# Sums of squares for the norms: from GpSimd to ScalarE and VectorE in a two-part transformer block

## The chip, the cores and the metric

The program runs on one NeuronCore of a Trainium2 chip. The metric is the device time of one execution in microseconds, the median of several. Times below are microseconds (us) unless marked ns. PE is TensorE's matmul, PEld its weight load, DVE is VectorE, ACT is ScalarE, POOL is GpSimd, SP is SyncE, which only issues DMAs here.

## The reference

One sequence of 512 tokens with 1024 channels, in float32, goes through two blocks of two layers each. What matters here is the residual stream and the norm that follows every addition to it:

```python
def rms_norm(x, g):
    xf = x.astype(jnp.float32)
    y = xf * lax.rsqrt(jnp.mean(xf * xf, axis=-1, keepdims=True) + EPS)
    return (y * g.astype(jnp.float32)).astype(x.dtype)

# first block: convolution, feed-forward, attention, feed-forward
h = h + conformer_conv(h, ...)            # pw2 is its last product
h = h + swiglu_ffn(h, ...)                # ffn_out
h = h + nsa_attention(h, ...)             # w_o
h = h + swiglu_ffn(h, ...)
return rmsnorm(h, final_norm)
# second block, for each of two layers
h = rms_norm(x, g_mix[layer])
x = x + mixer(h, ...)                     # e_w_out in layer 0, o_w_out in layer 1
m = rms_norm(mem, g_mem[layer])
x = x + memory_cross_attention(rms_norm(x, g_xa[layer]), m, ...)   # xa_wo
x = x + swiglu(rms_norm(x, g_ffn[layer]), ...)                     # ffn2_out
```

## The kernel before, in words

The stream lies transposed in SBUF as `x`, eight tiles of 128 channels by 512 tokens. Float32 products are made of three float32r products (`three`): each operand is split into a high and a low part. A weight panel (128x1024) is loaded by SP into `raw`, ScalarE copies it into `wh` (L185), VectorE takes the rest into `wl` (L191). There are four panel slots, and the loads and splits run four panels ahead. Products go round a ring of four PSUM banks.

A `Residual` stage (L517) adds a product to the stream. TensorE makes eight products, one for each tile m. For tile m VectorE adds the PSUM bank to `x` (L644, with a bias L641), which frees the bank. ScalarE then writes `xh`, the high part of x times the next norm's gain (L620), and the high part of the panels that lie four ahead (L185). VectorE makes these panels' low part (L191) and last `xl`, the low part of x (L649). `xh` and `xl` of tile m let TensorE take block k = m of the first product of the next stage. In the stages pw2, w_o, e_w_out and o_w_out a product has 8 blocks and each tile takes one panel; in ffn_out it has 22 blocks and three panels; in xa_wo it has 4 blocks, and two tiles share a panel. Engines run their own instruction streams and meet at semaphores only; within an engine the order is as written, stage after stage (`plan`, L2344).

The norm's scale does not stand in the way of the product: the next stage multiplies the unscaled stream, and its result is scaled by `rstd` as it leaves PSUM. `Norm` gets `rstd` from `ssq`, the running sum over the eight tiles of x squared: after the first product of the next stage TensorE sums `ssq` over partitions (L377), ScalarE takes the root, VectorE the reciprocal (L404), and after the second product TensorE spreads it (L386) and VectorE copies it into `rstd` (L406).

`ssq` is made by GpSimd: it clears it (L598, once the norm before has read it), and for each tile squares x (L605) and adds (L609), behind VectorE's L644. Nine `Residual` stages do so, 72 tiles. `Prepare` (L288), which comes at the start and between the two blocks, has another split of the work: ScalarE writes `xh` (L314) and the square (L317), VectorE `xl` (L344), GpSimd only adds (L308). The second `Prepare` first applies the final norm on VectorE (L334). The stage before it, ffn_out1, has no gain: no `xh` and `xl` there, and TensorE goes straight to the sum (L377).

GpSimd has other work in its stream. In front of the e_w_out and the o_w_out stage stands `MemoryLoad`: it waits until its arena is free, starts the DMA of the memory tokens `mem_x` (L2155), waits for it, and squares and adds eight tiles of 128x256 (L2159, L2163). Only then come L598 and the sums of that stage:

```python
    def memory_attention(layer, free, w_out, mixer_parts, source):
        mem = Memory(c, layer, free, source)
        add(MemoryLoad(mem))
        res = add(Residual(c, w_out, mixer_parts, source, [KD], 1, ("g_xa", KD * layer)))
        norm = add(Norm(c, res))
```

Of the kernel before, what the change touches and what calls it, by code (L numbers as in the profile page):

```python
# [21 lines left out]
ALU = mybir.AluOpType  # L22
ACT = mybir.ActivationFunctionType
# [6 lines left out]
KD = D // P  # L30
# [58 lines left out]
def repeat(eng, n, body, straight=False, peel=0):  # L89

    if straight or n - peel == 1:
        peel = n
    for i in range(peel):
        body(i)
    if peel < n:
        with eng.Fori(peel, n) as i:
            body(i)
# [115 lines left out]
class Stage:  # L213
# [5 lines left out]
    def gpsimd(self, pool):  # L219
        pass  # L220

    def scalar(self, act):
        pass

    def vector(self, dve):
        pass
# [61 lines left out]
class Prepare(Stage):  # L288
# [11 lines left out]
    def gpsimd(self, pool):  # L300
        c = self.c
        if self.norm:
            pool.wait_ge(self.norm.stat.sem, self.norm.stat0 + 1)
        pool.memset(c.ssq[:], 0.0).then_inc(self.summed.sem, 1)
        for m in range(KD):
            pool.wait_ge(self.summed.sem, self.summed0 + 1 + m)
            pool.wait_ge(self.squared.sem, self.squared0 + m + 1)
            pool.tensor_tensor(c.ssq[:], c.ssq[:], c.square[:, m % 2, :], ALU.add).then_inc(self.summed.sem, 1)  # L308

    def scalar(self, act):  # L310
        c = self.c
# [29 lines left out]
    def low(self, dve, m):  # L341
        c = self.c
        dve.wait_ge(self.high.sem, self.high0 + m + 1)
        c.nc.vector.scalar_tensor_tensor(c.xl[:, m, :], c.x[:, m, :], c.col(*self.at(m)),  # L344
                                         c.xh[:, m, :].bitcast(F32), ALU.mult, ALU.subtract).then_inc(
            self.ready.sem, 1)


class Norm(Stage):
# [167 lines left out]
class Residual(Stage):  # L517
# [74 lines left out]
    def gpsimd(self, pool):  # L592
        c = self.c
        if self.last:
            return

        pool.wait_ge(self.norm.stat.sem, self.norm.stat0 + 1)
        pool.memset(c.ssq[:], 0.0).then_inc(self.summed.sem, 1)  # L598

        def turn(i):  # L600
            for m in range(self.body):
                at = bass.ds(self.body * i + m, 1)
                pool.wait_ge(c.banks_freed.sem, self.product0 + m + 1 + self.body * i)
                pool.wait_ge(self.summed.sem, self.summed0 + m + self.body * i)
                pool.tensor_tensor(c.square[:, m % 2, :].rearrange("p (a n) -> p a n", a=1), c.x[:, at, :],  # L605
                                   c.x[:, at, :], ALU.mult).then_inc(self.squared.sem, 1)
                pool.wait_ge(self.summed.sem, self.summed0 + 1 + m + self.body * i)
                pool.wait_ge(self.squared.sem, self.squared0 + m + 1 + self.body * i)
                pool.tensor_tensor(c.ssq[:], c.ssq[:], c.square[:, m % 2, :], ALU.add).then_inc(self.summed.sem, 1)  # L609
        repeat(pool, self.turns, turn)  # L610

    def scalar(self, act):
        c = self.c

        def turn(i):
            for m in range(self.body):
                if self.gain:
                    at = bass.ds(self.body * i + m, 1)
                    act.wait_ge(c.banks_freed.sem, self.product0 + m + 1 + self.body * i)
                    c.nc.scalar.activation(c.xh[:, at, :], c.x[:, at, :], ACT.Copy,  # L620
                                           scale=c.col(self.gain[0], self.gain[1] + m + self.body * i)).then_inc(
                        self.high.sem, 1)
                for j in self.panels_of(m):
                    c.ahead(c.split_high, act, self.panel0, j, i, self.body_panels)
        repeat(act, self.turns, turn, straight=self.last)

    def vector(self, dve):
        c = self.c

        def turn(i):  # L630
            for m in range(self.body):
                at = bass.ds(self.body * i + m, 1)
                last = (m // self.pack * len(self.cuts)) + len(self.cuts)
                if m % self.pack == self.pack - 1:
                    dve.wait_ge(c.panels_used.sem, self.panel0 + last + self.body_panels * i)
                else:
                    dve.wait_ge(self.within.sem, self.within0 + m // self.pack + 1)
                bank = (self.product0 + m) % RING_BANKS
                out = c.psum[:, bank:bank + 1, :]
                if self.bias:  # L640
                    dve.scalar_tensor_tensor(c.x[:, at, :], out, c.col(self.bias, m + self.body * i), c.x[:, at, :],  # L641
                                             ALU.add, ALU.add).then_inc(c.banks_freed.sem, 1)
                else:
                    dve.tensor_tensor(c.x[:, at, :], out, c.x[:, at, :], ALU.add).then_inc(c.banks_freed.sem, 1)  # L644
                for j in self.panels_of(m):
                    c.ahead(c.split_low, dve, self.panel0, j, i, self.body_panels)
                if self.gain:
                    dve.wait_ge(self.high.sem, self.high0 + m + 1 + self.body * i)
                    dve.scalar_tensor_tensor(c.xl[:, at, :], c.x[:, at, :],  # L649
                                             c.col(self.gain[0], self.gain[1] + m + self.body * i),  # L650
                                             c.xh[:, at, :].bitcast(F32), ALU.mult, ALU.subtract).then_inc(
                        self.ready.sem, 1)
        repeat(dve, self.turns, turn, straight=self.last)


# [2037 lines left out]
```

## Time and profile before

| | |
|---|---|
| median of 3 runs | 2897.74 us (2897.13 to 2897.91) |
| span of the profiled execution | 2896.6 us |
| own time of the profiled execution | not given apart from its span; the median is 1.1 us above the span |
| PE, PEld busy | 2666.0 us (92%), 2158.2 us (75%) |
| DVE busy | 1473.0 us (51%) |
| ACT busy | 994.7 us (34%) |
| POOL busy | 370.3 us (13%), of it L605 84.0 us and L609 106.3 us |
| DMA | mean 77 GB/s |

The span is what one execution takes on the core; the table's shares are of the whole span and hide that the stages have different limits. In the timeline a row gives the start, the duration, the engine, the line, what is written and read, and in brackets how long the engine had been idle and which instruction ended that. Instructions of one engine overlap by some tens of ns, so that the next one's start comes a little before the end of the last.

### The profile page before, as it was taken

To read this page: it belongs to the slowest core of one execution; us is meant where nothing else is said; L and a number is where in the kernel's file an instruction comes from. 1 tells how busy PE (TensorE), PEld (TensorE's weight loads), DVE (VectorE), ACT (ScalarE), POOL (GpSimd) and SP (SyncE) were. 2 spreads that over 40 slices of the span, in tenths; PEclk is the share of its full clock that TensorE was granted. 3 is DMA by queue.
4 is the path that set the end of the run, shared out by engine and by line. 5 is a ranking of instruction groups with operands and counts; after the bars stand their busy time and mean duration, and the time that the engine had idled before them with its cause. 6 is when DMAs were issued, how large, how long until landed. Compare 5 with 4: busy or idle time off the path is not lost.

```text
span 2896.6 us, 36377 instructions
## 1 busy us (share of the span) xinstructions
PE 2666.0 (92%) x12452; PEld 2158.2 (75%) x12452; DVE 1473.0 (51%) x2499; ACT 994.7 (34%) x1658; POOL 370.3 (13%) x314
## 2 busy tenths in 40 slices
PE   6677999999878899999989889899999999899999
PEld 5534888877767778888757778588888778588887
DVE  4996444335566645443444455544433565544422
ACT  5523333223357733222233443323322223422321
POOL 3761100011000020001220031200001041200000
PEclk9888999999779999999989899999999999899999
DMA  4201333224300013332322014023323333133321
GB/s 141 70 0 31 98 95 94 75 100 135 99 1 1 1 58 102 94 97 80 105 67 74 22 36 124 22 92 97 92 80 103 99 94 109 30 94 99 93 97 66
DMA packets 61356, 222.42 MB, mean 77 GB/s; under 512 B 7232, under 2 KB 7488, under 8 KB 60624
## 3 DMA queue, kind: packets, MB, share of 16 engines
q1 hardware_dynamic: 58896, 209.15, 23.7%
q0 software_dynamic: 2368, 12.06, 1.3%
q8 instruction: 55, 0.90, 0.1%
q14 instruction: 37, 0.30, 0.0%
HBM read 216.47 MB, written 2.10 MB: 75 GB/s over the span
## 4 chain that ended last, share of the span: by engine, by line
PE 81%; DVE 11%; ACT 3%; issue 3%; DMA 1%; ACTq 0%; DVEq 0%; POOL 0%; SPq 0%; POOLq 0%
PE psum L208 23%; PE psum L210 23%; PE psum L209 23%; DVE conv_out L736 4%; PE psum L1657 3%; DVE wl L191 1%; PE psum L1644 1%; ACT wh L185 1%; PE psum L1082 1%; PE psum L1030 1%; PE psum L1671 1%; DVE xl L344 1%; PE psum L1672 1%; DVE xl L649 1%; DVE x L644 1%
## 5 line engine op out<-in xcount | busy, mean ns | idle before, releaser
L208 PE MATMUL psum<-xh,wh 128*128 128x512 f32 x1880 | 745.5, 397 | 55.1 <-DVE wl L191 22.8
L209 PE MATMUL psum<-xl,wh 128*128 128x512 f32 x1880 | 740.0, 394 | 0.0
L210 PE MATMUL psum<-xh,wl 128*128 128x512 f32 x1880 | 739.4, 393 | 0.0
L185 ACT ACTIVATE wh<-raw 128x1024 fp32r<-128x1024 f32 x404 | 422.8, 1056 | 875.8 <-PE psum L210 869.6
L191 DVE TENSOR_TENSOR wl<-raw,wh 128x1024 fp32r<-128x1024 f32 x404 | 543.7, 1358 | 249.4 <-ACT wh L185 249.3
L208 PEld LDWEIGHTS psum<-xh,wh 128*128 128x128 f32 x1880 | 356.8, 190 | 139.2 <-issue 27.6
L210 PEld LDWEIGHTS psum<-xh,wl 128*128 128x128 f32 x1880 | 356.8, 190 | 76.8 <-issue 0.9
L209 PEld LDWEIGHTS psum<-xl,wh 128*128 128x128 f32 x1880 | 357.1, 190 | 74.4 <-issue 0.6
L605 POOL TENSOR_TENSOR square<-x 128x512 f32 (+1 forms) x72 | 84.0, 1167 | 1600.6 <-DVE x L644 1506.8
L208 PE MATMUL psum<-hidden_high,wh 128*128 128x512 f32 x704 | 278.3, 395 | 0.0
L210 PE MATMUL psum<-hidden_high,wl 128*128 128x512 f32 x704 | 278.1, 395 | 0.0
L209 PE MATMUL psum<-hidden_low,wh 128*128 128x512 f32 x704 | 278.0, 395 | 0.0
L644 DVE TENSOR_TENSOR x<-psum,x 128x512 f32 (+1 forms) x72 | 49.6, 688 | 324.5 <-PE psum L210 324.3
L497 DVE TENSOR_TENSOR up<-psum,rstd 128x512 f32<-128x512 f32 x96 | 66.3, 691 | 266.4 <-PE psum L210 266.4
L620 ACT ACTIVATE xh<-x,cols (+1 forms) x64 | 46.4, 724 | 363.4 <-DVE x L644 332.9
L208 PEld LDWEIGHTS psum<-hidden_high,wh 128*128 128x128 f32 x704 | 132.2, 188 | 33.7 <-DVE wl L191 2.2
L210 PEld LDWEIGHTS psum<-hidden_high,wl 128*128 128x128 f32 x704 | 132.2, 188 | 31.9
L209 PEld LDWEIGHTS psum<-hidden_low,wh 128*128 128x128 f32 x704 | 132.3, 188 | 31.3
L736 DVE SCALAR_TENSOR_TENSOR conv_out<-conv_in,cols,conv_out 128x512 f32<-128x512 f32 x120 | 120.8, 1077 | 0.0
L478 ACT ACTIVATE hidden_high<-up 128x512 f32 x88 | 55.6, 632 | 175.7 <-DVE up L508 175.7
L609 POOL TENSOR_TENSOR ssq<-ssq,square 128x512 f32<-128x512 f32 x72 | 106.3, 1476 | 8.0
L490 DVE TENSOR_TENSOR pre<-psum,rstd 128x512 f32<-128x512 f32 x96 | 66.4, 691 | 79.2 <-PE psum L210 78.0
(356 smaller groups left out, 3429.3 us busy)
## 6 DMA issues: line engine op xcount, KB each, us to landing
raw<-ffn_in SPq DMA_DIRECT2D x176, 512.0 KB, 3.5
raw<-ffn_out SPq DMA_DIRECT2D x64, 448.0 KB, 4.1
raw<-ffn_out SPq DMA_DIRECT2D x32, 512.0 KB, 3.6
raw<-pw SPq DMA_DIRECT2D x24, 512.0 KB, 3.6
raw<-o_w_hgg SPq DMA_DIRECT2D x12, 512.0 KB, 4.2
raw<-w_q SPq DMA_DIRECT2D x8, 512.0 KB, 4.4
raw<-w_o SPq DMA_DIRECT2D x8, 512.0 KB, 3.5
raw<-e_w_qk SPq DMA_DIRECT2D x8, 512.0 KB, 3.6
```

Source lines behind the costliest of these rows:

```text
L185: self.nc.scalar.activation(self.wh[:, slot, :], self.raw[:, slot, :], ACT.Copy).then_inc(self.weights_high.sem, 1)
L191: self.nc.vector.tensor_tensor(self.wl[:, slot, :], self.raw[:, slot, :], self.wh[:, slot, :].bitcast(F32), ALU.subtract).then_inc(self.we ...
L208: nc.tensor.matmul(out, ah, bh, start=start, stop=False)
L209: nc.tensor.matmul(out, ah, bl, start=False, stop=False)
L210: return nc.tensor.matmul(out, al, bh, start=False, stop=stop)
L490: dve.tensor_tensor(c.pre[:, r, :], c.psum[:, bank, :], c.rstd[:], ALU.mult).then_inc(c.banks_freed.sem, 1)
L497: dve.tensor_tensor(c.up[:, r, :], c.psum[:, bank, :], c.rstd[:], ALU.mult).then_inc(c.banks_freed.sem, 1)
L605: pool.tensor_tensor(c.square[:, m % 2, :].rearrange("p (a n) -> p a n", a=1), c.x[:, at, :], c.x[:, at, :], ALU.mult).then_inc(self.squar ...
L609: pool.tensor_tensor(c.ssq[:], c.ssq[:], c.square[:, m % 2, :], ALU.add).then_inc(self.summed.sem, 1)
L644: dve.tensor_tensor(c.x[:, at, :], out, c.x[:, at, :], ALU.add).then_inc(c.banks_freed.sem, 1)
L736: dve.scalar_tensor_tensor(out, taps, w, out, ALU.mult, ALU.add).then_inc(self.tapped.sem, 1)
L1657: mm = pe.matmul(c.psum[:, 1 + u % 2, 0:P], self.pt_sb[u % 4][:, t * P:(t + 1) * P], vals, start=(t == 0), stop=(t == i))
```

## The change

GpSimd keeps only the clearing of `ssq`. In `Residual`, ScalarE squares tile m right behind `xh` and before it splits panels, and VectorE adds the square at the end of its work on tile m, behind `xl`. In the stage without gain ScalarE now waits for x (banks_freed) before it squares, in front of the panels. ScalarE's loops of the `Residual` stages are written out. In `Prepare`, VectorE adds behind each `xl`.

```diff
 class Prepare(Stage):
     def gpsimd(self, pool):
...
         pool.memset(c.ssq[:], 0.0).then_inc(self.summed.sem, 1)
-        for m in range(KD):
-            pool.wait_ge(self.summed.sem, self.summed0 + 1 + m)
-            pool.wait_ge(self.squared.sem, self.squared0 + m + 1)
-            pool.tensor_tensor(c.ssq[:], c.ssq[:], c.square[:, m % 2, :], ALU.add).then_inc(self.summed.sem, 1)
...
     def low(self, dve, m):
...
+        dve.wait_ge(self.summed.sem, self.summed0 + 1 + m)
+        dve.wait_ge(self.squared.sem, self.squared0 + m + 1)
+        dve.tensor_tensor(c.ssq[:], c.ssq[:], c.square[:, m % 2, :], ALU.add).then_inc(self.summed.sem, 1)

 class Residual(Stage):
     def gpsimd(self, pool):
...
         pool.wait_ge(self.norm.stat.sem, self.norm.stat0 + 1)
         pool.memset(c.ssq[:], 0.0).then_inc(self.summed.sem, 1)
-        def turn(i):
-            for m in range(self.body):
-                at = bass.ds(self.body * i + m, 1)
-                pool.wait_ge(c.banks_freed.sem, self.product0 + m + 1 + self.body * i)
-                pool.wait_ge(self.summed.sem, self.summed0 + m + self.body * i)
-                pool.tensor_tensor(c.square[:, m % 2, :].rearrange("p (a n) -> p a n", a=1), c.x[:, at, :],
-                                   c.x[:, at, :], ALU.mult).then_inc(self.squared.sem, 1)
-                pool.wait_ge(self.summed.sem, self.summed0 + 1 + m + self.body * i)
-                pool.wait_ge(self.squared.sem, self.squared0 + m + 1 + self.body * i)
-                pool.tensor_tensor(c.ssq[:], c.ssq[:], c.square[:, m % 2, :], ALU.add).then_inc(self.summed.sem, 1)
-        repeat(pool, self.turns, turn)
...
     def scalar(self, act):
...
+                if not self.last:
+                    at = bass.ds(self.body * i + m, 1)
+                    if not self.gain:
+                        act.wait_ge(c.banks_freed.sem, self.product0 + m + 1 + self.body * i)
+                    act.wait_ge(self.summed.sem, self.summed0 + m + self.body * i)
+                    c.nc.scalar.activation(c.square[:, m % 2, :].rearrange("p (a n) -> p a n", a=1), c.x[:, at, :],
+                                           ACT.Square).then_inc(self.squared.sem, 1)
                 for j in self.panels_of(m):
                     c.ahead(c.split_high, act, self.panel0, j, i, self.body_panels)
-        repeat(act, self.turns, turn, straight=self.last)
+        repeat(act, self.turns, turn, straight=True)
...
     def vector(self, dve):
...
+                if not self.last:
+                    dve.wait_ge(self.summed.sem, self.summed0 + 1 + m + self.body * i)
+                    dve.wait_ge(self.squared.sem, self.squared0 + m + 1 + self.body * i)
+                    dve.tensor_tensor(c.ssq[:], c.ssq[:], c.square[:, m % 2, :], ALU.add).then_inc(self.summed.sem, 1)
```

GpSimd's stream in front of the o_w_out stage, as it stood. `mem_sq` and `mem_sum` are the memory tokens' squares and their sum:

```order
L2159 TENSOR_TENSOR mem_sq<-mem_x 128x256
L2163 TENSOR_TENSOR mem_sum<-mem_sum,mem_sq 128x256 [waits mem_summed,mem_squared]
L598 MEMSET ssq 128x512 [waits stat]
L96 UNCONDITIONAL_BRANCH
L96 ISA
L604 REGISTER_ALU [waits banks_freed]
L605 ISA [waits summed]
L605 TENSOR_TENSOR square<-x 128x512
L607 REGISTER_ALU
L608 REGISTER_ALU [waits summed]
L609 TENSOR_TENSOR ssq<-ssq,square 128x512 [waits squared]
```

And as it stands now:

```order
L2158 TENSOR_TENSOR mem_sq<-mem_x 128x256
L2162 TENSOR_TENSOR mem_sum<-mem_sum,mem_sq 128x256 [waits mem_summed,mem_squared]
L2158 TENSOR_TENSOR mem_sq<-mem_x 128x256
L2162 TENSOR_TENSOR mem_sum<-mem_sum,mem_sq 128x256 [waits mem_summed,mem_squared]
L597 MEMSET ssq 128x512 [waits stat] x2
```

The squares and sums are gone; the clearing of `ssq` still stands behind the memory tokens' squares, and so does the clearing for the stage after (the x2).

VectorE's stream at the first tile of the o_w_out stage, before:

```order
L2101 TENSOR_TENSOR oy_low<-hgg,oy_high 128x512 [waits pc_high] x4
L96 UNCONDITIONAL_BRANCH
L96 ISA
L644 ISA [waits panels_used]
L644 TENSOR_TENSOR x<-psum,x 128x512
L190 REGISTER_ALU
L191 TENSOR_TENSOR wl<-raw,wh 128x1024 [waits weights_high]
L648 REGISTER_ALU
L649 ISA [waits x_high]
L649 SCALAR_TENSOR_TENSOR xl<-x,cols,xh 128x512
L635 REGISTER_ALU
L644 ISA [waits panels_used]
```

And now:

```order
L639 ISA [waits panels_used]
L639 TENSOR_TENSOR x<-psum,x 128x512
L190 REGISTER_ALU
L191 TENSOR_TENSOR wl<-raw,wh 128x1024 [waits weights_high]
L643 REGISTER_ALU
L644 ISA [waits x_high]
L644 SCALAR_TENSOR_TENSOR xl<-x,cols,xh 128x512
L649 REGISTER_ALU
L650 REGISTER_ALU [waits summed]
L651 TENSOR_TENSOR ssq<-ssq,square 128x512 [waits squared]
L630 REGISTER_ALU
L639 ISA [waits panels_used]
```

Between `xl` of one tile and the addition to x of the next stands the addition to `ssq`, which waits for the semaphore `summed`; for the first tile that is the clearing on GpSimd.

ScalarE's stream there, before (inside a loop) and after:

```order
L620 ISA [waits banks_freed]
L620 REGISTER_ALU
L620 ACTIVATE xh<-x,cols 128x512
L183 ISA
L86 REGISTER_ALU [waits landed0]
L185 ACTIVATE wh<-raw 128x1024 [waits panels_used]
```

```order
L608 ACTIVATE xh<-x,cols 128x512 [waits banks_freed]
L616 ACTIVATE square<-x 128x512 [waits summed]
L185 ACTIVATE wh<-raw 128x1024 [waits panels_used,landed0]
L608 ACTIVATE xh<-x,cols 128x512 [waits banks_freed]
L616 ACTIVATE square<-x 128x512 [waits summed]
```

The square has come in between `xh` and the panel's high part, and the register work of the loop is gone.

## Rows read from the trace of the kernel before

**Rows 1.** The page, shares by engine in the chain that ended last.

```profile
PE 81%; DVE 11%; ACT 3%; issue 3%; DMA 1%; ACTq 0%; DVEq 0%; POOL 0%; SPq 0%; POOLq 0%
```

**Rows 2.** Timeline of the first 60 us: start, duration, engine, line.

```profile
7.67 0.61 ACT L317 ACTIVATE square<-x 128x512 f32<-128x512 f32 x1
...
7.89 0.75 DVE L344 SCALAR_TENSOR_TENSOR xl<-x,cols,xh 128x512 fp32r<-128x512 f32 x1 [7.89 <-ACT xh L314]
...
20.28 5.69 DVE L191 TENSOR_TENSOR wl<-raw,wh 128x1024 fp32r<-128x1024 f32 x4
```

**Rows 3.** Line 191 in the first 40 us: ns min/median/max.

```profile
L191 DVE TENSOR_TENSOR wl<-raw,wh x5: 1210/1211/2283, 20.3 to 39.8; 128x1024 fp32r<-128x1024 f32 x5
```

**Rows 4.** Timeline around the first xa_wo stage, VectorE and then ScalarE.

```profile
1856.18 0.69 DVE L644 TENSOR_TENSOR x<-psum,x 128x512 f32<-128x512 f32 x1 [0.44 <-PE psum L210]
...
1863.37 0.68 DVE L644 TENSOR_TENSOR x<-psum,x 128x512 f32<-128x512 f32 x1
1865.78 2.33 DVE L191 TENSOR_TENSOR wl<-raw,wh 128x1024 fp32r<-128x1024 f32 x1 [1.74 <-ACT wh L185]
...
1883.20 0.74 DVE L649 SCALAR_TENSOR_TENSOR xl<-x,cols,xh 128x512 fp32r<-128x512 f32 x1
...
1895.96 0.69 DVE L406 COPY rstd<-psum 128x512 f32<-128x512 f32 x1 [8.31 <-PE psum L386]
...
1899.28 1.23 DVE L191 TENSOR_TENSOR wl<-raw,wh 128x1024 fp32r<-128x1024 f32 x1
1900.42 0.69 DVE L508 TENSOR_TENSOR up<-up,pre 128x512 f32<-128x512 f32 x1
...
1864.08 0.72 ACT L620 ACTIVATE xh<-x,cols 128x512 fp32r<-128x512 f32 x1 [1.54 <-DVE x L644]
1864.71 1.04 ACT L185 ACTIVATE wh<-raw 128x1024 fp32r<-128x1024 f32 x1
```

**Rows 5.** Timeline of VectorE at the end of the w_o stage.

```profile
1066.65 0.69 DVE L644 TENSOR_TENSOR x<-psum,x 128x512 f32 x1 [0.56 <-PE psum L210]
...
1071.02 0.74 DVE L649 SCALAR_TENSOR_TENSOR xl<-x,cols,xh  x1
1072.25 0.69 DVE L644 TENSOR_TENSOR x<-psum,x 128x512 f32 x1 [0.49 <-PE psum L210]
```

**Rows 6.** Timeline from ffn_out1's last tile into the second Prepare, VectorE and then TensorE.

```profile
1437.52 0.69 DVE L644 TENSOR_TENSOR x<-psum,x 128x512 f32 x1 [9.37 <-PE psum L210]
...
1447.76 2.08 DVE L334 SCALAR_TENSOR_TENSOR x<-x,cols,rstd 128x512 f32<-128x512 f32 x3
...
1442.49 1.86 PE L377 MATMUL psum<-mean,ssq 128*128 128x1 f32 x8 [5.13 <-POOL ssq L609]
...
1464.30 0.79 PE L208 MATMUL psum<-xh,wh 128*128 128x512 f32 x1 [1.72 <-DVE xl L344]
```

**Rows 7.** Timeline of the o_w_out stage, VectorE and then GpSimd.

```profile
2402.00 0.74 DVE L649 SCALAR_TENSOR_TENSOR xl<-x,cols,xh  x1
...
2411.07 0.69 DVE L406 COPY rstd<-psum 128x512 f32<-128x512 f32 x1 [6.01 <-PE psum L386]
...
2360.08 1.60 POOL L2159 TENSOR_TENSOR mem_sq<-mem_x 128x256 f32<-128x256 f32 x1 [4.46 <-DMA mem_x<-memT]
...
2375.12 0.53 POOL L598 MEMSET ssq<- 128x512 f32 x1
```

**Rows 8.** Timeline of the e_w_out stage, VectorE and then GpSimd.

```profile
1759.50 0.74 DVE L649 SCALAR_TENSOR_TENSOR xl<-x,cols,xh  x1
...
1712.52 0.61 POOL L2159 TENSOR_TENSOR mem_sq<-mem_x 128x256 f32<-128x256 f32 x1 [4.29 <-DMA mem_x<-memT]
...
1724.93 0.53 POOL L598 MEMSET ssq<- 128x512 f32 x1
```

**Rows 9.** Windows at ffn_out0's end: length, busy PE, PEld, DVE, ACT, POOL, PEclk, DMA, GB/s.

```profile
669.90:672.70 2.80, 0.04 (x1) 0.00 (x0) 2.80 (x3) 1.21 (x1) 0.00 (x0) 1.00 0.65 189
672.70:685.00 12.30, 12.24 (x48) 10.29 (x49) 0.87 (x4) 3.43 (x5) 0.00 (x0) 0.72 0.23 86
```

## The prediction

> **What bounds the kernel now.** First I read the shares of the chain that ended last: TensorE holds 81% of it, VectorE 11%, GpSimd 0% [rows 1]. GpSimd's squares and additions are therefore no time to be won by themselves. They can only count where TensorE waits: at a stage's end, where its next product needs the last tile's `xl`. So I read next the timelines around each such place, asking what `xl` waited for, and where GpSimd slowed VectorE. That it does is plain: the same panel split takes 1.21 us alone and up to 2.28 us while GpSimd adds [rows 3], 2.33 us in xa_wo against 1.23 us a little later [rows 4].
>
> **Step times.** From [rows 4], read start to start: x to `xh` 0.71 us where ScalarE has no loop (so everywhere after the change); `xh` to the next ScalarE instruction 0.63; `wh` to VectorE's `wl` 1.07; `wl` to the next 1.14 alone. A square lasts 0.61 [rows 2], less the 0.09 of overlap that `xh` shows (0.72 long, 0.63 to the next): 0.52. VectorE's instructions overlap by the same 0.09 (1.23 long, 1.14 to the next): `xl` 0.65 (0.74 long), and the new addition, priced as L508, also of two SBUF inputs, 0.60 (0.69 long). The new chain from x to the end of `xl` is 0.71+0.63+0.52+1.07+1.14+0.74 = 4.81 us, and from one x to the next, when VectorE is behind, 0.71+0.63+0.52+1.07+1.14+0.65+0.60 = 5.32 us. A product of 8 blocks takes 1072.25-1066.65 = 5.60 us [rows 5].
>
> **The parts, from the start of the program to its end.**
>
> *Start.* VectorE's eight `xl` and four `wl` lie before the first matmul. `wl` starts at 20.28 and, held up by GpSimd, ends 2.28 later, at 22.56 [rows 2, 3]. Now eight times 0.65+0.60 from 7.89 gives 17.9, and `wl` alone ends at 19.1. **-3.4 us.** The eight added additions cost 4.8 us there, and what is gained is more.
>
> *pw2 and w_o.* The last x to the end of `xl` took 1071.02+0.74-1066.65 = 5.11 us, now 4.81: what the square adds to the chain, the vanished contention and ScalarE's loop give back. TensorE needs it seven blocks into the next product, 7/8 of 5.60 = 4.9 us, so it waited a little and now hardly does. **-0.3 each, -0.6.** In the middle of the stage VectorE's 5.32 stay under the product's 5.60, so nothing builds up.
>
> *ffn_out0 and ffn2_out0.* The same edits, with three panels in the chain; between them 15 us of product hide everything but the last tile. TensorE stood still for 2.8 us there [rows 9]. **-0.3 each, -0.6.**
>
> *ffn_out1 and the second Prepare.* GpSimd's sum was complete at 1442.49, when TensorE's sum began [rows 6]. Now ScalarE cannot split its panels early: it waits for x, squares, then splits; VectorE adds behind three `wl`. From x at 1437.52: 0.71+0.52+1.07+3x1.14+0.69 = 6.41, so 1443.93, 1.5 us later. Then the first new x starts at 1447.76+1.5 = 1449.26; three x take 2.0; then five rounds of `xl`, addition, x at 0.65+0.60+0.65 = 1.90, and the sixth `xl` ends at 1461.5. TensorE, which started its last nine matmuls on it at 1464.30, starts them at 1461.6. **-2.7 us** in all, the 1.5 included.
>
> *o_w_out.* Here the change adds a wait. VectorE's first addition needs the cleared `ssq`, and GpSimd clears only behind the memory tokens. It began these at 2360.08 and cleared at 2375.12 [rows 7]; before, GpSimd alone was late for that, and caught up. Now VectorE stands, and behind it in its stream stand all further additions to x. Standing, it no longer holds up GpSimd: the same sixteen instructions with one pair held up took 1724.93-1712.52 = 12.41 us [rows 8], against 15.04 here with three. So clearing starts at 2372.5, ends at 2373.0, the second tile's x starts at 2373.6. Six steps of 5.32 later comes the last, at 2405.5, and its `xl` ends at 2410.3, against 2402.74. The lag cannot be worked off, since a step is only 0.28 us shorter than a product. TensorE itself is not held inside the stage: tile 1's bank and panel are needed only four products (22 us) after its own product, and they come with a lag of 11 us. It is held in the next stage's first product, at blocks 6 and 7. **+7.6 us.** Were GpSimd no faster for VectorE's standing, the clearing would stay at 2375.12 and this part be +10.2; I take the former, since with one pair held up instead of three its row is there. The Trainium skill (SBUF — State Buffer, section "SBUF: two separate sides") calls the port pair that VectorE and GpSimd share an exclusive lock, which a VectorE instruction with two SBUF inputs holds for its whole length. By that rule a standing VectorE frees GpSimd at once, which makes +7.6, and the split's 2.33 against 1.23 us [rows 4] agrees with it.
>
> *e_w_out.* The same, but the memory tokens came early: the clearing starts at 1724.93 [rows 8], ends at 1725.5, the second x starts at 1726.1, the last at 1758.0, its `xl` ends at 1762.8 against 1760.24. **+2.6 us.**
>
> *TensorE's clock.* After the 2.8 us of standing at ffn_out0's end the granted clock was 0.72 over the next 12.3 us, that is at 1.2 instead of 2.4 GHz for a part of it [rows 9]. Its price I read from the time between the last `xl`'s end and the copy of `rstd`: 9.07 us counted from the start of `xl` at 2402.00 to 2411.07, where the clock held [rows 7], against 1895.96-1883.20 = 12.76 after xa_wo [rows 4]: 3.7 us. The window at ffn_out0 gives (1-0.72)x12.3 = 3.4 us. Both memory stages will now make TensorE stand about as long as ffn_out0 does, or longer. I take 3.0 for each, between 0 (e_w_out's clock may hold) and 3.7. **+6.0 us.**
>
> *xa_wo, twice.* VectorE was the bound there already. First tile of a pair: 0.71+0.72+0.65+0.60 = 2.68 to the next x; second: 5.32; a pair 8.0 us. From the second tile's x at 1856.18 three pairs later is 1880.2, and `xl` ends at 1885.0 against 1883.94 [rows 4]. The added work is more than the contention. **+1.1 each, +2.2.**
>
> GpSimd's queue otherwise: its DMAs come no later than before, SP's loads hang on `wl`, which follows the steps above.
>
> **Sum.** -3.4-0.6-0.6-2.7+7.6+2.6+6.0+2.2 = **+11.1 us** on the span of 2896.6, so 2907.7; the median of the runs is 1.1 above that span, and I give **2908.8**.
>
> **Rivals.** *(1) The waits at the clearing cost nothing and the rest is a small gain.* For it speaks that four banks and four panels do cover TensorE inside the stage. It holds if VectorE works off its lag: 7.6 us in six steps needs steps 1.3 us shorter than I count, 4.0 in place of 5.3. Then o_w_out, e_w_out and the clock drop out: 11.1-16.2 = -5.1, 2892.6 us. Against it stands the chain of five dependent steps, each with a row. That would be a result not slower; with a Start or Prepare gain 1 us larger it is faster beyond what can be measured.
>
> *(2) Only part of it: TensorE's clock holds after e_w_out and falls for a short time after o_w_out,* so the clock costs 1.5 in place of 6.0, and the clearing in e_w_out hides in the ring: 11.1-4.5-2.6 = +4.0, 2901.7, which no measurement tells from no change.
>
> *(3) A VectorE step takes over 5.60 us.* The loops of VectorE stay, their register work and two more waits may not hide, and x to `xh` may keep the loop's larger gap: 0.4 us would do. Then pw2 and w_o fall behind by 0.2 a tile, 1.3 us each in place of -0.3, the memory stages by 2.5 more each, and the clock falls at two more places: 11.1+3.2+5+6 = +25, 2923 us. It decides from a step of 5.60 on. At 5.5 it costs only 1 us in each memory stage.
>
> That the change does not do what it says can be left out: the order of instructions shows the work gone from GpSimd and present on the others.
>
> **Chances.** Forecast 0.68; rival 1 0.10; rival 2 0.12; rival 3 0.10. The range takes in the clock (0 to 3.7 at each place), the clearing (up to +2.6), a step up to 5.5, a Start gain down to half, and the upper part of rival 2: 2901 to 2917. 0.2%, 5.8 us, is about what a measurement of this kernel tells from no change. Slower than that: the forecast but for its lowest end and rival 3, 0.79; within: rival 2 and most of rival 1, 0.16; faster: 0.05.
>
> **What would show it.** In the profile after: the first `wl` near 17.9; on VectorE an idle time of some 10 us before the first addition of o_w_out and 3 to 4 before that of e_w_out, ended by GpSimd's clearing; x to x at 5.3 in what follows; TensorE waiting some 9 us for `xl` in the first product of the next stage; a granted clock well below 1.00 in the 10 us after both; xa_wo pairs at 8.0. Wrong I would be above all if the steps after the clearing were shorter than 5.0 us, or if TensorE did not wait for `xl` behind these two stages.

## The result and the profile after

| | before | after |
|---|---|---|
| median of 7 runs each | 2897.74 us (2896.33 to 2901.06) | 2906.57 us (2903.26 to 2912.94) |
| ratio | | 1.0028, 95% interval 1.0017 to 1.0038 |
| span of the profiled execution | 2896.6 us | 2911.2 us (its own time 2912.94, the highest of the seven) |

Slower by 8.8 us, where 11.1 had been forecast. The profiled execution is 6.4 us slower than the changed kernel's median, so a second profile of it (e5 below) is read beside the first.

The page after: busy time by engine, and the shares in the chain that ended last, against [rows 1]:

```profile
PE 2674.6 (92%) x12452; PEld 2165.8 (74%) x12452; DVE 1452.4 (50%) x2587; ACT 1030.2 (35%) x1730; POOL 153.0 (5%) x154
...
PE 77%; DVE 12%; ACT 5%; issue 4%; DMA 1%; POOL 0%; DVEq 0%; ACTq 0%; SPq 0%; POOLq 0%
```

GpSimd lost 217 of its 370 us. VectorE's busy time did not rise but fell by 21 us although it makes 88 additions more: its other instructions are no longer held up. The 404 panel splits alone (`wl`, L191) went from 543.7 to 493.2 us. None of that is time of the kernel; TensorE lost 4 points of the chain to the others.

**Where the time went, stage by stage.** The copy of `rstd` (L406 before, L405 after) comes once behind each stage that makes a sum. Its start in the timelines, as difference from the one before it, minus the same difference in the kernel before, gives each stage's own part (us). The changed kernel has two columns, `after` and `e5`, which are two executions of one program: where they differ, the table shows scatter and not the change. The other columns are the experiments below:

| stage | forecast | after | e5 (after, again) | e1 | e8 | e7 | e4 | e6 |
|---|---|---|---|---|---|---|---|---|
| start | -3.4 | -3.7 | -3.0 | -2.7 | -3.6 | -4.2 | -2.6 | -3.0 |
| pw2 | -0.3 | -0.8 | -0.1 | -0.2 | -0.4 | -1.4 | -0.9 | -0.9 |
| ffn_out0 | -0.3 | -0.4 | -2.0 | -2.0 | -0.4 | -2.6 | -4.2 | -4.2 |
| attention, w_o | -0.3 | +3.5 | -2.5 | +1.9 | +3.4 | -3.1 | -2.1 | -2.1 |
| ffn_out1 | +1.5 | +1.5 | +1.5 | +1.5 | +1.5 | +1.4 | -1.5 | -1.5 |
| second Prepare | -4.2 | -4.7 | -5.2 | -4.5 | -4.6 | -5.2 | -4.6 | -4.7 |
| e_w_out | +2.6 +3.0 | +5.5 | +5.6 | -0.1 | +5.5 | -0.7 | -0.5 | -0.3 |
| xa_wo, layer 0 | +1.1 | +1.8 | +2.5 | +0.8 | +0.8 | +0.1 | -5.9 | -6.3 |
| ffn2_out0 | -0.3 | -0.1 | -1.6 | -0.1 | -1.7 | -2.3 | -0.7 | -2.3 |
| o_w_out | +7.6 +3.0 | +10.9 | +9.9 | -0.1 | -1.3 | -2.0 | -1.6 | -2.7 |
| xa_wo, layer 1 | +1.1 | +1.0 | +2.7 | +1.8 | +2.3 | +0.2 | -5.6 | -6.0 |

The o_w_out stage after, VectorE and then GpSimd, against [rows 7]:

```profile
2359.76 0.69 DVE L639 TENSOR_TENSOR x<-psum,x 128x512 f32 x1 [2.67 <-PE psum L210]
...
2363.85 1.10 DVE L644 SCALAR_TENSOR_TENSOR xl<-x,cols,xh  x1
2375.85 0.69 DVE L651 TENSOR_TENSOR ssq<-ssq,square 128x512 f32<-128x512 f32 x1 [10.90 <-POOL ssq L597]
2376.46 0.68 DVE L639 TENSOR_TENSOR x<-psum,x 128x512 f32 x1
...
2362.81 1.60 POOL L2158 TENSOR_TENSOR mem_sq<-mem_x 128x256 f32<-128x256 f32 x1 [4.57 <-DMA mem_x<-memT]
...
2375.20 0.53 POOL L597 MEMSET ssq<- 128x512 f32 x1
```

VectorE's first addition stands 10.9 us, and the second tile's x behind it starts 2376.46-2359.76 = 16.7 us after the first, where a product takes 5.6. GpSimd's pass over the memory tokens takes 2375.20-2362.81 = 12.39 us, where 12.41 had been forecast, against 15.04 before.

The timeline at the end of that stage, VectorE and TensorE:

```profile
2408.57 0.68 DVE L639 TENSOR_TENSOR x<-psum,x 128x512 f32 x1
...
2412.65 0.74 DVE L644 SCALAR_TENSOR_TENSOR xl<-x,cols,xh  x1
...
2413.44 0.80 PE L208 MATMUL psum<-xh,wh 128*128 128x512 f32 x1 [3.69 <-DVE xl L644]
...
2424.62 0.69 DVE L405 COPY rstd<-psum 128x512 f32<-128x512 f32 x1 [7.52 <-PE psum L385]
```

From the second x to the eighth, (2408.57-2376.46)/6 = 5.35 us a step. TensorE waited for `xl` at block 6 (4.38 us) and block 7 (the 3.69 shown), 8.07 us together.

The first x of e_w_out and of this stage in the kernel before:

```profile
1716.14 0.69 DVE L644 TENSOR_TENSOR x<-psum,x 128x512 f32 x1 [4.36 <-PE psum L210]
2357.36 0.69 DVE L644 TENSOR_TENSOR x<-psum,x 128x512 f32 x1 [2.88 <-PE psum L210]
```

From the first x to the last `xl` the stage now takes 2412.65-2359.76 = 52.89 us, against 2402.00-2357.36 = 44.64 before: 8.25 us of lag. From the start of the last `xl` to the copy it is 2424.62-2412.65 = 11.97 us, where it was 9.07 before: the 2.9 us more are TensorE's clock, as the windows show, at e_w_out and at o_w_out (length, busy PE, PEld, DVE, ACT, POOL, PEclk, DMA, GB/s):

```profile
1757.68:1769.50 11.82, 11.03 (x44) 9.40 (x45) 1.54 (x5) 0.75 (x3) 0.52 (x1) 0.72 0.16 46
2412.65:2424.70 12.05, 11.26 (x45) 9.56 (x46) 1.60 (x5) 0.63 (x2) 0.52 (x1) 0.71 0.15 44
```

The same stretches of the kernel before:

```profile
1759.50:1768.60 9.10, 9.07 (x48) 7.46 (x47) 0.94 (x4) 0.63 (x2) 0.53 (x1) 1.00 0.20 59
2402.00:2411.10 9.10, 8.30 (x44) 7.15 (x45) 0.94 (x4) 0.63 (x2) 0.53 (x1) 1.00 0.20 58
```

A granted clock of 0.71 is a mix of the levels 2.4 and 1.2 GHz.

e_w_out after, VectorE and then GpSimd, against [rows 8]:

```profile
1711.41 0.69 DVE L639 TENSOR_TENSOR x<-psum,x 128x512 f32 x1 [4.36 <-PE psum L210]
...
1720.89 0.69 DVE L651 TENSOR_TENSOR ssq<-ssq,square 128x512 f32<-128x512 f32 x1 [3.97 <-POOL ssq L597]
...
1757.68 0.74 DVE L644 SCALAR_TENSOR_TENSOR xl<-x,cols,xh  x1
...
1707.83 0.61 POOL L2158 TENSOR_TENSOR mem_sq<-mem_x 128x256 f32<-128x256 f32 x1 [4.33 <-DMA mem_x<-memT]
```

From the first x to the last `xl` it is 1757.68-1711.41 = 46.27 us, against 1759.50-1716.14 = 43.36 before: 2.9 us of lag.

What was won, at the start, against [rows 2, 3]: four `wl` now take 4.62 us, 1.21 each, and start 1.78 us earlier though eight additions stand before them.

```profile
18.50 4.62 DVE L191 TENSOR_TENSOR wl<-raw,wh 128x1024 fp32r<-128x1024 f32 x4
```

And what TensorE waited for longest in ffn_out1 and the second Prepare, against [rows 6]:

```profile
1436.09 0.69 DVE L639 TENSOR_TENSOR x<-psum,x 128x512 f32 x1 [8.97 <-PE psum L210]
...
1442.57 1.86 PE L376 MATMUL psum<-mean,ssq 128*128 128x1 f32 x8 [6.64 <-DVE ssq L651]
```

### The profile page after: what moved, and what is told of

Same layout as the page of the kernel before. It is cut to its first block, busy times and chain, and to the rows that moved or that the text cites. A ratio compares the mean times of both kernels' runs of the same rounds, so it can differ in the third digit from the quotient of the medians.

```text
span 2911.2 us, 35945 instructions
## 1 busy us (share of the span) xinstructions
PE 2674.6 (92%) x12452; PEld 2165.8 (74%) x12452; DVE 1452.4 (50%) x2587; ACT 1030.2 (35%) x1730; POOL 153.0 (5%) x154
## 4 chain that ended last, share of the span: by engine, by line
PE 77%; DVE 12%; ACT 5%; issue 4%; DMA 1%; POOL 0%; DVEq 0%; ACTq 0%; SPq 0%; POOLq 0%
PE psum L208 22%; PE psum L209 22%; PE psum L210 22%; DVE conv_out L735 4%; PE psum L1656 3%; ACT wh L185 1%; PE psum L1643 1%; DVE xl L644 1%; PE psum L1081 1%; DVE x L639 1%; DVE wl L191 1%; DVE ssq L651 1%; ACT square L616 1%; PE psum L1029 1%; PE psum L1670 1%
## 5 line engine op out<-in xcount | busy, mean ns | idle before, releaser
L191 DVE TENSOR_TENSOR wl<-raw,wh 128x1024 fp32r<-128x1024 f32 x404 | 493.2, 1234 | 281.8 <-ACT wh L185 281.8
L608 ACT ACTIVATE xh<-x,cols 128x512 fp32r<-128x512 f32 x64 | 46.3, 724 | 348.5 <-DVE x L639 321.9
L511 DVE TENSOR_TENSOR hidden_low<-up,hidden_high 128x512 f32 x88 | 60.9, 692 | 81.7 <-ACT hidden_high L477 81.7
L1656 PE MATMUL psum<-values,sparse_pt 128*128 128x128 f32 x640 | 99.9, 289 | 1.9 <-DVE o L1800 0.9
```

Source lines behind the costliest of these rows:

```text
L191: self.nc.vector.tensor_tensor(self.wl[:, slot, :], self.raw[:, slot, :], self.wh[:, slot, :].bitcast(F32), ALU.subtract).then_inc(self.we ...
L511: dve.tensor_tensor(self.hidden[1][:, at, :], c.up[:, r:r + 1, :], self.hidden[0][:, at, :].bitcast(F32), ALU.subtract).then_inc(self.read ...
L1656: mm = pe.matmul(c.psum[:, 1 + u % 2, 0:P], self.pt_sb[u % 4][:, t * P:(t + 1) * P], vals, start=(t == 0), stop=(t == i))
```

## The experiments

The theory behind the forecast (theory A below; B, C and D are its rivals): the change wins some 6 us by what it takes off GpSimd, and loses more where VectorE, put behind GpSimd's late clearing of `ssq`, gathers lag that its step of 5.35 us cannot work off against a product of 5.60. Rivals: the loss sits in the longer step itself, in `Prepare`, or in the attention. e1 to e4 share 16 runs of the kernel before, 2897.97 us (2893.84 to 2901.77); e5 to e8 share 13, 2898.23 (2895.71 to 2902.72).

**e1: `ssq` cleared ahead of the memory tokens.** The clearing becomes a method, and the two memory stages' `MemoryLoad` calls it before it waits for `mem_x`:

```diff
...
         pool.memset(self.sum[:], 0.0).then_inc(self.summed.sem, 1)
+        self.res.clear(pool)
         pool.wait_ge(self.loaded.sem, self.s[0] + 16)
...
```

> The changed kernel, but GpSimd clears ssq for the e_w_out and o_w_out stages before it squares the memory tokens, right after it has started their DMA. Theory A (the loss is VectorE's wait at the clearing): VectorE stands under 0.1 us before its first addition in both stages, TensorE waits there no longer than in w_o, its clock holds at both places (the time from the start of the last xl to the copy of rstd is 9.1 us again), so 7.6+2.6+6 us of my sum and 0.3 each more go: 2906.6-16.8, about 2890 us, faster than before by 8. Rival B (the longer steps of ScalarE and VectorE are what costs, and the clearing only lets it be seen): the time stays above 2902 us.

Measured 2890.11 us (11 runs), ratio 0.9974 (0.9965 to 0.9983), 16.5 us under the changed kernel. In its trace the clearing precedes the stage's first x (GpSimd, then VectorE):

```profile
2350.24 0.55 POOL L603 MEMSET ssq<- 128x512 f32 x1
...
2351.75 0.69 DVE L644 TENSOR_TENSOR x<-psum,x 128x512 f32 x1 [2.58 <-PE psum L210]
```

The copies of `rstd` give -0.1 at both stages, in place of +5.5 and +10.9: these add to 16.4, so the place of one memset of 0.53 us is the whole loss, and more. From the last `xl` to the copy it takes 9.03 and 9.09 us there, as in the kernel before: the clock holds. The time is A's 2890, and B's 2902 falls. The kernel is now 7.9 us below the one before, a small difference, but its interval lies below 1.

**e2 and e3: the change's halves.** e2 is the kernel before with the new `Prepare` alone; e3 the kernel before with the new `Residual` alone.

The whole edit of e2, in `Prepare`'s `gpsimd` and `low`; e3 is the rest of the change:

```diff
...
         pool.memset(c.ssq[:], 0.0).then_inc(self.summed.sem, 1)
-        for m in range(KD):
-            pool.wait_ge(self.summed.sem, self.summed0 + 1 + m)
-            pool.wait_ge(self.squared.sem, self.squared0 + m + 1)
-            pool.tensor_tensor(c.ssq[:], c.ssq[:], c.square[:, m % 2, :], ALU.add).then_inc(self.summed.sem, 1)
...
+        dve.wait_ge(self.summed.sem, self.summed0 + 1 + m)
+        dve.wait_ge(self.squared.sem, self.squared0 + m + 1)
+        dve.tensor_tensor(c.ssq[:], c.ssq[:], c.square[:, m % 2, :], ALU.add).then_inc(self.summed.sem, 1)
```

> The kernel before with only the two Prepare stages changed: VectorE adds there, GpSimd still squares and adds in the residual stages. Theory A: start -3.7 us and second Prepare -4.7 us as between the two traces, nothing else moves: 2897.7-8.4, about 2889 us. Rival C (in Prepare, too, the additions only take the place of the contention, and the gain seen in one trace is TensorE's clock by chance): 2896 us or more.

> The changed kernel with the two Prepare stages as before, so GpSimd adds there. Theory A: the changed kernel plus the 8.4 us of the Prepare stages, about 2915 us, slower than before by 17. If the parts did not add up (rival C), it would lie at 2907 to 2909 us.

e2: 2888.62 us (6 runs), ratio 0.9970 (0.9958 to 0.9982). e3: 2916.01 us (5 runs), ratio 1.0061 (1.0047 to 1.0075). The halves are -9.4 and +18.0; together +8.7, what the whole change shows, and C falls in both. So `Prepare`'s half is a gain by itself. The copies put -4.0 at the start and -5.2 in the second `Prepare` of e2, and in e3 +4.8 at e_w_out and +10.9 at o_w_out. In e2's profile 4.4 us more are won in the e_w_out part, where nothing was edited. That is TensorE's clock: the windows from copy to copy, before and in e2, have the same number of matmuls, 4.3 us less of TensorE's busy time, and a granted clock of 0.95 in place of 0.94:

```profile
1476.19:1768.59 292.40, 264.14 (x1347) 219.70 (x1346) 134.38 (x250) 106.77 (x201) 34.34 (x36) 0.94 0.18 55
```

```profile
1465.92:1753.96 288.04, 259.87 (x1347) 216.64 (x1346) 133.30 (x249) 106.80 (x201) 35.46 (x36) 0.95 0.18 55
```

**e5: the changed kernel, a second profile.** No edit.

> The changed kernel unaltered, for a second profile. Theory A: the extra time that its first profile shows between the copy of rstd behind ffn_out0 and the one behind w_o (404.9 us against 401.5 in the kernel before, 403.3 and 401.2 in two other variants) is TensorE's clock moving by chance, so it will be another number between 401 and 405 here, while o_w_out keeps its 10.9 us over before and e_w_out its 5.5, each within 1 us. Rival B: the change itself costs 3.5 us in the attention, and it is 404.9 again, within 0.3.

One run of 2906.86 us. Attention and w_o took 1077.98-679.01 = 398.97 us: B's 404.9 falls, and A's bounds of 401 to 405 were too narrow by 2. The windows over 900 to 950 us, of after and then of e5, show what differs, PEclk:

```profile
900.00:950.00 50.00, 41.94 (x290) 38.26 (x290) 29.12 (x183) 35.95 (x105) 0.00 (x0) 0.90 0.00 1
```

```profile
900.00:950.00 50.00, 41.09 (x314) 37.03 (x312) 32.15 (x203) 39.38 (x114) 0.00 (x0) 1.00 0.00 1
```

The windows over the whole stage, of after and of e5, settle how much of the 6 us it is:

```profile
679.32:1084.26 404.94, 353.59 (x2285) 302.96 (x2284) 236.06 (x950) 217.75 (x523) 7.57 (x15) 0.89 0.15 45
```

```profile
679.01:1077.98 398.97, 347.40 (x2285) 297.09 (x2284) 235.56 (x949) 217.88 (x523) 7.60 (x15) 0.91 0.15 46
```

The same 2285 matmuls take 6.2 us more of TensorE's time at the lower clock, and the stage is 6.0 us longer. One program thus moves by 6 us in this one stage, and TensorE's clock is all of it.

o_w_out gives +9.9 and e_w_out +5.6, within A's 1 us of 10.9 and 5.5. VectorE in e5, first x, last `xl` and copy of e_w_out and then of o_w_out:

```profile
1703.12 0.69 DVE L639 TENSOR_TENSOR x<-psum,x 128x512 f32 x1 [4.36 <-PE psum L210]
...
1749.51 0.74 DVE L644 SCALAR_TENSOR_TENSOR xl<-x,cols,xh  x1
...
1762.82 0.69 DVE L405 COPY rstd<-psum 128x512 f32<-128x512 f32 x1 [8.85 <-PE psum L385]
...
2351.13 0.69 DVE L639 TENSOR_TENSOR x<-psum,x 128x512 f32 x1 [2.88 <-PE psum L210]
...
2403.67 0.74 DVE L644 SCALAR_TENSOR_TENSOR xl<-x,cols,xh  x1
...
2415.99 0.69 DVE L405 COPY rstd<-psum 128x512 f32<-128x512 f32 x1 [7.86 <-PE psum L385]
```

From the first x to the last `xl` they took 46.39 and 52.54 us, so the lag was 3.0 and 7.9, nearly as in the first profile. The last `xl` to the copy took 13.31 and 12.32 us, so the clock cost 4.2 and 3.3. What makes the copies' sum nearly the same all the same is that the first x came 1.6 and 1.3 us sooner behind the copy before it than in the kernel before, which is no part of the lag.

**e8: the early clearing at o_w_out alone.** The edit is against e1.

```diff
...
-        self.res.clear(pool)
+        if self.res.early:
+            self.res.clear(pool)
...
-        res.early, mem.res = True, res
+        res.early, mem.res = layer == 1, res
...
```

> The changed kernel with the early clearing in the o_w_out stage alone; in e_w_out it stays behind the memory tokens. Theory A: the two stages cost what their copies of rstd show, 5.5 us for e_w_out (some 2.6 of lag and 2.9 of TensorE's clock falling behind it) and 10.9 for o_w_out, and they add up: 2890.1+5.5 = 2895.6. Rival B: the short wait at e_w_out costs nothing by itself and the clock falls there by chance: 2890 to 2892.

Measured 2896.60 us (10 runs), ratio 0.9992 (0.9982 to 1.0002): A's 2895.6, above B's 2890 to 2892. The last `xl` of its e_w_out and the copy behind it, in VectorE's timeline:

```profile
1758.14 0.74 DVE L649 SCALAR_TENSOR_TENSOR xl<-x,cols,xh  x1
...
1769.99 0.69 DVE L405 COPY rstd<-psum 128x512 f32<-128x512 f32 x1 [7.40 <-PE psum L385]
```

That is 11.85 us. The same time is 11.80 and 13.31 in the changed kernel's two profiles and 10.68 in e3, the four with lag behind e_w_out, and 9.03 to 9.58 in the six without (before, e1, e2, e4, e6, e7). In all ten profiles the clock falls behind e_w_out exactly where VectorE lags at its end, so it is not chance, as B had it.

**e7: the square behind the panels.** e1, with ScalarE squaring tile m after it has split the panels, and VectorE's sum left behind `xl`. `square` and `sum` are methods now that hold the waits and the instruction of the change, and VectorE's loops are written out too, so this run has two edits in it:

```diff
...
-                if not self.last:
...
+                if not self.last and not self.gain:
+                    self.square(act, self.body * i + m)
                 for j in self.panels_of(m):
                     c.ahead(c.split_high, act, self.panel0, j, i, self.body_panels)
+                if not self.last and self.gain:
+                    self.square(act, self.body * i + m)
...
-        repeat(dve, self.turns, turn, straight=self.last)
+        repeat(dve, self.turns, turn, straight=True)
...
```

> The clearing early as in e1, ScalarE's square behind its panels as in e4, but VectorE's sum behind xl as in the changed kernel. Theory A (square and sum each lengthen the chain by their own length wherever VectorE is the bound): the square's 0.52 us goes out of each step and of each last chain, a pair in xa_wo takes 7.5 in place of 8.1 and the xa_wo stages win 2.4 us each, the four stages with one panel a tile up to 0.5 each: 2890.1-4.9-2.1 = about 2883, and what is left to e4 (2868.4) is the sum's place. Rival B (only the square, which holds up the panels, counts, and the sum hides wherever it stands): about 2868 to 2872. Rival C (only the sum's place counts): 2888 to 2891.

Measured 2878.17 us (2873.60 to 2879.72, 4 runs), ratio 0.9929 (0.9912 to 0.9945). That is 5 us below A's figure and outside both rivals, so neither the square alone nor the sum alone is what counts. The xa_wo pairs came nearly as expected (7.5), 7.58 us against 8.10 in e1 (x to the next pair's x). The 0.52 us are just what the square had been counted at, so the written-out loops gave nothing there:

```profile
1840.86 0.69 DVE L654 TENSOR_TENSOR x<-psum,x 128x512 f32<-128x512 f32 x1
...
1848.44 0.69 DVE L654 TENSOR_TENSOR x<-psum,x 128x512 f32<-128x512 f32 x1
```

From the first x to the last `xl` the xa_wo stages take 29.1 us against 31.2 in e1, 2.1 less each where A had said 2.4. By the copies they give only 0.8 and 1.6 less, because what lies before the first x and behind the last `xl` moved too. ffn2_out0 and o_w_out give 2 less each, and the attention 5 less, which is within the 6 that e5 shows as its scatter. So the terms that A named came; that the total is 5 us lower still is not explained by them.

**e4: and the sum in the gap.** e7, with VectorE adding the square of tile m-1 right behind x of tile m, where it waits for ScalarE anyway, and only the last sum behind `xl`. In ffn_out1 the sum stands right behind x and the square ahead of the panels. The edit is against e7.

```diff
...
                     dve.tensor_tensor(c.x[:, at, :], out, c.x[:, at, :], ALU.add)
+                t = self.body * i + m
+                if not self.last and (t or not self.gain):
+                    self.sum(dve, t - 1 if self.gain else t)
                 for j in self.panels_of(m):
                     c.ahead(c.split_low, dve, self.panel0, j, i, self.body_panels)
...
-                if not self.last:
-                    self.sum(dve, self.body * i + m)
+                if not self.last and self.gain and self.body * i + m == KD - 1:
+                    self.sum(dve, KD - 1)
...
```

> As the kernel with the early clearing, and in the residual stages ScalarE squares behind the panels and not before, VectorE adds tile m-1 right behind x of tile m, while it would wait for ScalarE's panel anyway, and only the last tile behind xl; in the stage without gain it adds right behind x; VectorE's loops are written out. Theory A (the chain x, xh, square, wh, wl, xl, addition is the bound where VectorE is behind, above all in xa_wo): the chain from x to the end of xl falls from 4.8 to 4.3 us, a pair of xa_wo tiles from 8.1 to 6.3, and the sum of the stage without gain comes 4.3 us earlier: 16 to 18 us below the kernel with the early clearing, about 2873 us. Rival D (TensorE's wait is set by the product, the order inside a step is hidden): within 3 us of the kernel with the early clearing.

Measured 2868.39 us (2868.15 to 2873.52, 4 runs), ratio 0.9906 (0.9891 to 0.9921): 29.6 us under the kernel before, 9.8 under e7. D falls. Against e1 it is 21.7 us, where A had said 16 to 18; the attention gives 4.0 of it, which is within its scatter. The xa_wo stages now win 5.9 and 5.6 us on the kernel before. Of the 5.9, 4.3 are steps (first x to last `xl` 25.49 us against 29.82), and 2.1 are the clock behind them (10.64 us to the copy against 12.76), less 0.6 before the first x. ffn_out1 wins 1.5 where it had lost 1.5, so its sum came 3.0 us earlier and not 4.3 as A had it.

**e6: e4 with the clearing late again.** The order of e4, the memset back behind the memory tokens, where the changed kernel has it:

```diff
...
-        self.res.clear(pool)
...
-        res.early, mem.res = True, res
...
```

> The order of e4 (square behind the panels, sum of the tile before right behind x), but the clearing left where the changed kernel has it, behind the memory tokens. Theory A (what the late clearing costs is lag that VectorE cannot work off because its step, 5.35 us, is as long as a product, 5.60): here the chain from x to the next x is 0.71+0.63+1.07+1.14+0.65 = 4.20 us, so VectorE, which stands until some 16 us behind the first x of o_w_out and then has about 7 us of lag at the third x, works off 1.4 us a tile, and none is left at the last: 2868 to 2872 us, the same as e4 within 4. Rival B (the wait itself costs, wherever it lies): 2868.4+16.5 = about 2885.

Measured 2866.52 us (2865.27 to 2867.80, 4 runs), ratio 0.9894 (0.9877 to 0.9910). Rival B's 2885 falls. The wait is there, nearly as long as in the changed kernel, but one tile later: VectorE adds to the second x first. VectorE at o_w_out, the first addition with its wait, the next steps, and the last:

```profile
2330.65 0.69 DVE L654 TENSOR_TENSOR x<-psum,x 128x512 f32<-128x512 f32 x1 [2.63 <-PE psum L210]
...
2346.14 0.69 DVE L635 TENSOR_TENSOR ssq<-ssq,square 128x512 f32<-128x512 f32 x1 [9.20 <-POOL ssq L603]
2346.75 1.22 DVE L191 TENSOR_TENSOR wl<-raw,wh 128x1024 fp32r<-128x1024 f32 x1
2347.88 0.75 DVE L662 SCALAR_TENSOR_TENSOR xl<-x,cols,xh 128x512 fp32r<-128x512 f32 x1
2348.55 0.69 DVE L654 TENSOR_TENSOR x<-psum,x 128x512 f32<-128x512 f32 x1
...
2352.78 0.68 DVE L654 TENSOR_TENSOR x<-psum,x 128x512 f32<-128x512 f32 x1
...
2369.85 0.69 DVE L654 TENSOR_TENSOR x<-psum,x 128x512 f32<-128x512 f32 x1
...
2383.00 0.69 DVE L405 COPY rstd<-psum 128x512 f32<-128x512 f32 x1 [5.97 <-PE psum L385]
```

Here 9.2 us of standing cost nothing. The third x comes 17.90 us behind the first, 6.7 later than two products of 5.60 want it; the steps are 4.23 us; the eighth comes 39.20 us behind the first, seven products exactly. Two things differ from the changed kernel. The wait stands one tile later, so the lag behind it is 6.7 us and not the 16.70-5.60 = 11.1 there, and the step is 4.23 us and not 5.35. An estimate from these rows parts them: five steps of 5.35 work off 5x0.25 = 1.3 us and would leave 5.4 of the 6.7, five of 4.23 can work off 6.9 and leave none. With the changed kernel's lag of 11.1 even six steps of 4.23 would leave 2.9. So the wait disappears by both together, and no run has the one without the other.

## Why the prediction was right

**Start**, -3.4: -3.7 and -3.0. The first `wl` came at 18.50, not 17.9, but the first `xl` had come at 8.38 instead of 7.89, since the input `x` landed that much later; between them lie 10.12 us, against the 10.0 counted. The first matmul began at 19.97 where it had begun at 22.82, 2.85 us earlier, and with the 0.49 of the late start this is 3.34. The copy of `rstd` comes 3.7 us earlier and not 2.85; the 0.9 more lie behind the first matmul and were not taken apart.

**ffn_out1 and the second `Prepare`**, +1.5 and -4.2: +1.5 in both profiles and -4.7, -5.2. The sum matmul began 1442.57-1436.09 = 6.48 us after x, against 6.41 counted. TensorE began its last nine matmuls 24.18 us after that x in the first profile, where 24.1 had been counted and the kernel before had 26.78. So the term was right to 0.1 us, and the 0.5 and 1.0 beyond it are the clock: from there to the copy it took 11.89 us before, 11.35 and 10.79 in the two profiles of the change, at a granted clock of 0.81, 0.84 and 0.92.

**The clearing**, +7.6 and +2.6: from the first x to the last `xl`, +8.25 and +2.9 in the first profile, +7.9 and +3.0 in the second, so both terms were 0.3 to 0.7 us short. The choice between +7.6 and +10.2 rested on whether a standing VectorE frees GpSimd: the pass took 12.39 us, where 12.41 had been taken. GpSimd's squares took 0.61 us each while VectorE stood, and the one beside VectorE's work 1.60. The exclusive lock that the Trainium skill describes (SBUF — State Buffer, section "SBUF: two separate sides") agrees with these rows.

**The clock**, +3.0 each: 2.9 and 2.7, then 3.3 and 4.2. The price had been read from places where TensorE already stood, and it carried over, though the 4.2 lies above the upper bound of 3.7. TensorE waited 8.07 us for `xl`, where some 9 had been said.

**xa_wo**, +1.1 each, pairs of 8.0: +1.8 and +1.0, then +2.5 and +2.7, pairs of 8.1. From the first x to the last `xl`, which is what the term was counted from, all four are alike: 31.2 us against 29.8 before, 1.35 more. So the term was 0.3 short, three pairs 0.1 us longer each; the rest of the copies' spread lies before the first x and behind the last `xl`.

**The step**, 5.32: 5.35. Rival 3 needed 5.60; with ScalarE's loops written out no gap was left. (Its price was a little high: 0.4 us more makes 5.72, only 0.12 over a product and not 0.2.) Rival 1 (waits that cost nothing) asked for steps of 4.0; they were 5.35, so it was rightly put low, and e6 shows that its condition was the right kind: at 4.23, with the wait one tile later, it costs nothing. Rival 2 (the clock holds behind e_w_out, and the clearing there hides) failed in both profiles of the change.

**The small terms**, -0.3 each (pw2, w_o, ffn_out0, ffn2_out0): the copies scatter by more than this, but the last x of a stage and the last `xl`'s end lie close together and show it. They went from 5.17 to 4.89 us at pw2, from 5.11 to 4.83 at w_o, from 7.38 to 7.11 at ffn_out0 and from 7.32 to 7.11 at ffn2_out0, and are within 0.02 us of that in e5. All four were right.

**What the forecast left out**: that the attention moves by 6 us between two executions of the same kernel. Its range was built from the terms alone and had no room for this. The two profiles of the change lie on either side of the kernel before there, 404.9 and 399.0 against 401.5 us, so this stage makes the total uncertain and not the account of it.

## What to carry to other kernels

When work moves to an engine further up the critical path, list for each moved instruction what it now waits for, and ask where in its new engine's order it stands: what is queued behind it inherits the wait. What is left of a wait at the stage's end is the lag behind it, less the difference between pace and step for each step that remains: compute the step first (here 5.35 against 5.60, then 4.23) and the number of steps left to catch up. Cheap work belongs in a gap that the engine has anyway, one tile late, and not at the end of the chain that the next stage hangs on: the sum's place alone was worth 9.8 us (e7 to e4). Together with the square behind the panels and VectorE's loops written out it turned +8.8 us into -31.7, with the same work on the same engines.

When two profiles are compared, measure a term between the two instructions that it was counted from. First x to last `xl` at o_w_out gave 52.89 and 52.54 us in two executions of one program, while whole stages of it differed by up to 6.

## What the runs showed of the hardware

A memset of 0.53 us that stands behind 12 us of other work in GpSimd's order cost 16.5 us of kernel time. VectorE's busy time fell, 1473.0 to 1452.4 us, while it took on 88 additions of 0.68 us (60 us): some 80 us of its former busy time had been longer instructions beside GpSimd's, 50.5 us of them in the panel splits. One stage of one program differed by 6 us between two executions, with a granted clock of 0.89 and 0.91 over it and 6.2 us more of TensorE's busy time for the same 2285 matmuls; a difference under that in this stage of a single profile is no evidence.
